# A four-layer hybrid encoder trunk: an attention order in which two steps share one PSUM tile, a last projection over the stored tokens alone, and four state buffers in the gated recurrence

## The reference, cut to what matters

```python
for i in range(DEPTH):                       # DEPTH = 4
    a = rms_norm(h, norm_mix_g[i])
    y = [mla_mixer, hgrn2_mixer, s5_mixer, retention_mixer][i](a, ...)
    h = h + y
    f = conv_glu_ffn(rms_norm(h, norm_ffn_g[i]), ...)   # 1024 -> 2*2816 -> conv -> silu*gate -> 1024
    h = h + f
return h[:, N_META:]                         # N_META = 16

# layer 0, per head: q, k, v from low-rank latents, q and k normalised over 192 columns
s = einsum(q_block, k) * scale;  s = where(mask, s, NEG_INF);  o = softmax(s) @ v
# layer 1, per head, in chunks: gated linear recurrence
state = state * exp(g_last) + k_tail^T v;    o = q_dec @ state + masked(q_dec k_inv^T) v
o = rms_norm(o, g_o) * silu(g)
```

## Time and profile before

| | us |
|---|---|
| median of three runs | 3178.77 |
| the profiled execution | 3176.39 |
| its span | 3174.6 |
| PE busy | 2892.7 (91%) |
| DVE busy | 2079.7 (66%) |
| POOL busy | 1319.7 (42%) |
| ACT busy | 977.1 (31%) |

### The profile page before, as it was taken

One profiled execution on the slowest core, in us unless ns is written; L12 is line 12 of the kernel. 1 busy time (PEld: TensorE's weight loads), 2 busy tenths in 40 slices (PEclk: granted clock), 3 DMA queues, 4 the chain that ended last, 5 costly groups with the idle time before them and its releaser, 6 DMA issues.

```text
span 3174.6 us, 59011 instructions
## 1 busy us (share of the span) xinstructions
PE 2892.7 (91%) x23040; PEld 2750.6 (87%) x23040; DVE 2079.7 (66%) x2743; ACT 977.1 (31%) x1403; POOL 1319.7 (42%) x603
## 2 busy tenths in 40 slices
PE   6778899999888879998965799999999999999999
PEld 6566799999888879998965799999999898899999
DVE  5676478861576757888969568884235435688840
ACT  3222233332334323332235333333212122222221
POOL 4111245564222224554453245555434243255553
PEclk8789899999999989999977899999999999999999
DMA  3100122233211112222310122223332222122232
GB/s 127 34 27 26 47 74 90 85 102 99 75 49 50 53 47 74 87 84 87 94 62 1 34 81 86 84 88 107 118 93 68 75 93 72 49 74 85 86 107 79
DMA packets 66412, 234.51 MB, mean 74 GB/s; under 512 B 8145, under 2 KB 8913, under 8 KB 65777
## 3 DMA queue, kind: packets, MB, share of 16 engines
q1 hardware_dynamic: 63648, 225.70, 23.3%
q10 hardware_dynamic: 2640, 7.02, 0.7%
HBM read 230.60 MB, written 2.10 MB: 73 GB/s over the span
## 4 chain that ended last, share of the span: by engine, by line
PE 50%; DVE 31%; issue 13%; ACT 2%; DVEq 2%; POOL 2%; DMA 0%; SPq 0%; ACTq 0%; POOLq 0%
PE ps L225 38%; DVE scr L445 7%; DVE scr L448 7%; DVE ub L439 4%; DVE scr L442 3%; PE ps L247 2%; PE ps L1893 1%; PE ps L1384 1%; ACT work L1688 1%; DVEq L442 1%; DVE work L1064 1%; DVE work L811 1%; PE ps L1009 1%; PE ps L238 1%; PE ps L1369 1%
## 5 line engine op out<-in xcount | busy, mean ns | idle before, releaser
L225 PE MATMUL ps<-xs,wr 128*128 128x264 f32 x13056 | 1646.5, 287 | 53.9 <-POOL wr L213 34.9
L213 POOL TENSOR_TENSOR wr<-raw,wr 128x1024 fp32r<-128x1024 f32 x422 | 1087.7, 2581 | 1441.5 <-ACT wr L205 1440.9
L225 PEld LDWEIGHTS ps<-xs,wr 128*128 128x128 f32 x13056 | 1612.7, 191 | 83.2 <-issue 51.6
L225 PE MATMUL ps<-hid,wr 128*128 128x264 f32 x6528 | 803.7, 286 | 25.4 <-POOL wr L213 17.6
L225 PEld LDWEIGHTS ps<-hid,wr 128*128 128x128 f32 x6528 | 798.8, 190 | 29.2 <-POOL wr L213 19.6
L205 ACT ACTIVATE wr<-raw 128x1024 fp32r<-128x1024 f32 x422 | 441.4, 1050 | 416.9 <-PE ps L225 413.1
L448 DVE SCALAR_TENSOR_TENSOR scr<-ub,convp,scr 128x528 f32<-128x528 f32 x176 | 448.1, 2546 | 24.0 <-DVE scr L445 0.6
L445 DVE SCALAR_TENSOR_TENSOR scr<-ub,convp,scr 128x528 f32<-128x528 f32 x176 | 228.9, 1301 | 26.6 <-DVE scr L442 17.5
L513 POOL TENSOR_TENSOR hid<-scr,hid 128x528 f32 x88 | 137.3, 1560 | 232.7 <-ACT hid L485 232.7
L464 DVE TENSOR_TENSOR h<-ps,h 128x528 f32<-128x528 f32 x32 | 22.6, 708 | 308.0 <-PE ps L225 307.8
L485 ACT ACTIVATE hid<-scr 128x528 f32 x88 | 56.8, 646 | 408.6 <-DVE scr L454 408.6
(11 more groups left out here) (249 smaller groups left out, 2263.3 us busy)
## 6 DMA issues: line engine op xcount, KB each, us to landing
raw<-in_stream SPq DMA_DIRECT2D x422, 512.0 KB, 3.6
work<-in_ret_tab ACTq DMA_DIRECT2D x4, 1056.0 KB, 5.3
h<-in_h SPq DMA_DIRECT2D x8, 264.0 KB, 6.0
out<-h SPq DMA_DIRECT2D x8, 256.0 KB, 4.5
work<-in_s_b ACTq DMA_DIRECT2D x1, 512.0 KB, 3.5
work<-in_s_c ACTq DMA_DIRECT2D x1, 512.0 KB, 4.6
convp<-in_convp ACTq DMA_DIRECT2D x4, 88.0 KB, 2.2
work<-in_mla_tab ACTq DMA_DIRECT2D x1, 264.0 KB, 2.5
```

The lines of the kernel that those rows point to most:

```text
L213: pool.tensor_tensor(wr[:, s, 1].rearrange("p a b -> p (a b)"), raw[:, s, :], wr[:, s, 0].rearrange("p a b -> p (a b)").bitcast(F32), ALU. ...
L225: mm = pe.matmul(out[:, q], wr[:, slot, w, b0 + k], x[k][v][:, q * HALF:(q + 1) * HALF], start=start and k == 0 and p == 0, stop=stop and ...
```

## The change: what it does, and the diff

- **Attention.** The value transposes leave `sum` and become a step `vt` of their own with a tile of their own, behind `spreadk`. `sum` moves from behind `O1` to right behind `("S", 4)`, and it writes into the tile of `("S", 4)`, whose scores lie in the first 16 columns (`tile_of`). `vv` moves behind `O1`. The loop keeps 22 tiles.
- **Recurrence.** Four state buffers in place of one. The update is a DVE operation that reads the new part straight from PSUM in `("S", b)`; the copy to `us` and the update in `("O", b)` go. The order is new: `OM` and the elementwise steps `e1'`, `e2'` come earlier, `q'` later, `e3'` ahead of `i'`, and `e4'` ahead of `Q`. The square on ACT is a step `sq`. PE sums the squares within `g'`, after 18 of its 48 matmuls (`SPLIT = 3`).
- **Last MLP.** Its down projection computes columns 16 to 527 alone, with one matmul of 512 columns where there were two of 264 (`project_real`).

```diff
+        def project_real(pe, out, slot, x, start, stop, inc, before):
+            for k in range(len(x)):
+                if k in before:
+                    pe.wait_ge(*before[k])
+                for p, (w, v) in enumerate(((0, 0), (0, 1), (1, 0))):
+                    mm = pe.matmul(out[:, 0:SEQ], wr[:, slot, w, k], x[k][v][:, META:T],
+                                   start=start and k == 0 and p == 0, stop=stop and k == len(x) - 1 and p == 2)
+            mm.then_inc(inc, 1)
...
+                        if last:
+                            project_real(pe, flat(gg + m), u % RING, x, j == 0, j == 2, unit_done, before)
...
-            P_SEQ = ["qn", "qr", "kn", "vv", "sum", "spreadq", "spreadk"]
+            P_SEQ = ["qn", "qr", "kn", "sum", "vv", "spreadq", "spreadk", "vt"]
...
-            X_SEQ = [("S", 0), ("S", 1), "qn", ("T", 0), ("S", 2), "qr", ("O", 0), "kn", ("T", 1), ("S", 3),
-                     "vv", ("T", 2), ("S", 4), ("O", 1), "sum", ("T", 3), ("O", 2), ("T", 4), "spreadq",
-                     "spreadk", ("O", 3), ("O", 4)]
+            X_SEQ = [("S", 0), ("S", 1), "qn", ("T", 0), ("S", 2), "qr", ("O", 0), "kn", ("T", 1), ("S", 3), ("T", 2),
+                     ("S", 4), "sum", ("O", 1), "vv", ("T", 3), ("O", 2), ("T", 4), "spreadq", "spreadk", "vt",
+                     ("O", 3), ("O", 4)]
+            def tile_of(seq, k):
+                return k - (seq is X_SEQ and k >= seq.index("sum"))
...
-                    pe.wait_ge(tile_free, g - 3 + i * W2)
+                    if s != "sum" or g < gX:
+                        pe.wait_ge(tile_free, g - 3 + i * W2)
...
+                    elif s == "vt":
+                        dve.wait_ge(p_pe.sem, p_pe.done("vt", h0) + i * 2 * len(p_pe.names))
+                        dve.tensor_copy(vt[j][:, 0:512], flat(g)[:, 0:512]).then_inc(p_dve.sem, p_dve.one("vt"))
+                        dve.tensor_copy(vt[j][0:META, 512:512 + P], flat(g)[0:META, 512:512 + P]).then_inc(tile_free, 1)
...
-            state = misc[:, 128:256]
-            us = [ub[:, 1, 130:258], ub[:, 1, 258:386]]
+            state = [misc[:, 128:256]] + [b_["ms"][:, QUARTER + k * P:QUARTER + (k + 1) * P] for k in range(QB - 1)]
...
-            P_SEQ = ["f", "q", "e1", "e2", "i", "e3", "e4", "g", "e5"]
-            X_SEQ = ["VK", "M", "f'", ("S", 0), "q'", "OM", "e1'", ("S", 1), ("O", 0), ("S", 2), "e2'",
-                     ("O", 1), ("S", 3), "i'", ("O", 2), "e3'", ("O", 3), "Q", "e4'", "g'", "N", "F", "e5'"]
+            P_SEQ = ["f", "e1", "e2", "q", "e3", "i", "e4", "g", "e5"]
+            X_SEQ = ["VK", "M", "f'", "OM", ("S", 0), "e1'", "e2'", "q'", ("S", 1), ("O", 0), ("S", 2), ("O", 1), ("S", 3),
+                     "e3'", "i'", ("O", 2), ("O", 3), "sq", "e4'", "Q", "g'", "N", "F", "e5'"]
...
+                    if r and s == "g":
+                        project(pe, tile(g), slot, 0, x[:SPLIT], True, False)
+                        squares(i, g)
+                        project(pe, tile(g), slot, SPLIT, x[SPLIT:], False, True, unit_done)
...
-                        dve.wait_ge(p_act.sem, p_act.done("Et", R))
+                        dve.wait_ge(p_act.sem, p_act.done("sigq", R))
...
                         if b < QB - 1:
                             masked.then_inc(a_dve.sem, a_dve.one(("mk", b)))
+                            dve.wait_ge(tile_free, g_of(("S", b - 1) if b else "OM", g) + 1 + i * PER)
+                            dve.scalar_tensor_tensor(state[b + 1], state[b], d128[:, b:b + 1], f[:, 512:640], ALU.mult, ALU.add)\
+                               .then_inc(tile_free, 1)
                             dve.wait_ge(a_dve.sem, a_dve.done(("mk", b), R))
-                            dve.tensor_copy(us[b % 2], f[:, 512:640]).then_inc(tile_free, 1)
...
-                        if b < QB - 1:
-                            dve.scalar_tensor_tensor(state, state, d128[:, b:b + 1], us[b % 2], ALU.mult, ALU.add)\
-                               .then_inc(a_dve.sem, a_dve.one(("st", b)))
```

More of the change, by code:

```diff
@@ L392, in setup_of, with ffn_pe @@
             return mixer[n].get("setup") if n in mixer else None
-        def ffn_pe(pe, n, layer, u0, g0):
+        def ffn_pe(pe, n, layer, u0, g0, last):
             x = split_tiles(xs, range(DT))
@@ L422, in ffn_pe @@
                         pe.wait_ge(lo_ready, u + 1 + i * 12)
-                        project(pe, tile(gg + m), u % RING, 0, split_tiles(hid, range(k0, k0 + nb)),
-                                j == 0, j == 2, unit_done, {k - k0: w for k, w in late.items()})
+                        x, before = split_tiles(hid, range(k0, k0 + nb)), {k - k0: w for k, w in late.items()}
+                        if last:
+                            project_real(pe, flat(gg + m), u % RING, x, j == 0, j == 2, unit_done, before)
+                        else:
+                            project(pe, tile(gg + m), u % RING, 0, x, j == 0, j == 2, unit_done, before)
                         k0 += nb
```

106 lines of the change are left out of this document (62 added, 44 removed).

## The result

| kernel | median, us (lowest to highest, runs) | profiled execution, us | its span, us | mean granted clock |
|---|---|---|---|---|
| before | 3178.68 (3175.6 to 3180.93, 4) | 3176.39 | 3174.6 | 0.951 |
| after | 3128.12 (3123.69 to 3135.3, 4) | 3125.63 | 3123.5 | 0.954 |

The ratio after to before is 0.9846, 95% interval 0.9827 to 0.9865: 50.6 us less in the medians (43 to 55 by the interval), where 35.5 were forecast. The time of 3128 lies inside the range of 3110 to 3160, but outside the forecast's own 3134 to 3150, on the side of more gain.

The account below looks back on a forecast made before the run. Attention and recurrence were taken as chains of waits between PE and DVE, the last down projection as PE alone. Gains of 9.1, 18.8 and 7.6 us made 35.5 off 3176.39: 3140.9, median 3143; own range 3134 to 3150, whole 3110 to 3160.

Parts of the forecast that it names:

- rival 2: Recurrence: the split stops the roots but the clock holds, 1.9 us per head more gain, 3130 us; chance 0.12.
- constant extra per matmul: Last down projection: 10.6 ns per matmul whatever its width, so 223.9 ns for 512 columns and 9.1 us less.
- upper bound: Last down projection: the extra grows with the columns, 233.9 ns per 512-column matmul and 3.8 us less.
- Rival 4: Last down projection: the 512-wide matmul doesn't stream, 0.85 ns per column, slower than before at 3254 us; chance 0.04.
- The roots' start: Attention loop: roots start 1.38 us behind block 3's probabilities, 2.85 us earlier in the mean.
- the tile wait: Attention loop: `spreadq` waits for the tile of `vv`, freed about 0.9 us later than before.
- `vt` cost: Attention loop: the two `vt` copies between `spreadk` and the next `S0` cost 0.4 us per head.
- half of the heads makes 0.5: Attention loop: half of the heads have their spreads at full clock, worth 0.5 us per head.
- Rival 5: Attention: the new order fails through the `vv` tile wait or `O1`, 0 to 0.5 us per head, 3153 us; chance 0.06.
- my walk: Recurrence loop: step-by-step timing of one head, 35.0 us before the split's hold on the roots is charged.
- Rival 1: Recurrence: the split doesn't stop the roots, heads of 35.0 us, gain 38.4 us, 3112 us; chance 0.13.
- Rival 3: Recurrence gains nothing: a second split or longer low clock, 7.6 to 12 us less gain, 3151 to 3155; chance 0.10.

Follow-up runs that it names:

- e9: Late round's kernel with `vv` again ahead of block 2's transposes in the attention loop; 3103.95 us.
- e4: Changed kernel with ACT rounding the gate's weight unit only behind the gate's sigmoid in the recurrence; 3113.53 us, ratio 0.9798 to the kernel before.
- e6: Changed kernel with 20 extra matmuls of 264 columns on PE ahead of its wait for the roots in the recurrence loop; 3121.48 us, ratio 0.9838.
- the late round: Changed kernel with the recurrence's gate weight unit rounded on ACT behind the gate's sigmoid, not ahead; 3113.53 us, and 3113.13 us when run again.

## Why the forecast was right in sign and place, and too small

The number alone would mislead: 3128 lies beside rival 2's 3130, and its distance to the forecast is made of errors of both signs.

1. **The last projection: the term was mis-sized.** I took a constant extra per matmul (223.9 ns, 9.1 us). The extra grows with the columns: 231.1 ns, 5.0 us measured, near my upper bound of 233.9 ns and 3.8 us. The choice of a constant was made without a row of another width in a stream of this type; the proportional bound was the nearer one. Rival 4 (0.85 ns per column) didn't happen: 0.45.
2. **Attention, the loop: 2.0 us per head forecast, 2.4 in the mean of six: 3.2 in a head of 31.0 us and 1.5 in one of 32.7.** The roots' start was right (1.28 us behind the copy against 1.38), the tile wait too (0.90 against 0.9). `vt` cost 0.05 instead of 0.4. The other step that was too small is "half of the heads makes 0.5": the spreads are at full clock in six of seven, in none without the cover of `vv`. By e9 that cover is worth 1.5 us against a head of 31.0, and 0.7 in the mean of six heads. The three heads of 32.5 to 32.9 us have the low level at other places (one of them at its spreads, which take 3.88 us); that wasn't in the sum. Rival 5 had nothing to it.
3. **Attention, the ends.** The first head gained 5.9 us (4.8 forecast). Up to its spreads it is 4.9 us, as forecast (they start 15.3 us behind the start of `turn` before and 10.4 after). The other 1.0 us lies behind them, where the low level lasts until 108.6 before and until 101.1 after; that this is the cause was not tried. From the last loop head to the output projection it was 6.1 where one head's 2.0 was forecast: in the trace before the last score blocks ran at the low level, in the one after at the full one. I didn't price that stretch at all.
4. **The recurrence loop: right by the mechanism, too small by 4.5 us.** Heads of 39.4 us in the mean of the first four intervals (forecast 39.4), a root operation held to the end of the split, a pause of 3.10 us (3.5). e4 and e6 take the two terms away one by one: 2.2 us for the split, 1.7 to 2.2 for the clock (2.3 and 1.9 forecast), and what is left is the 35.0 us of my walk. Rival 1 was worth what I had for it and didn't occur. Rival 2 occurred at one pause of seven, and with it the last two intervals are 37.9 and 38.1 us; without them the stage would have gained 8 us. The first head of the loop gained 2.4 us from its `VK` to its `N`. That makes 14.3 us for the loop against the 9.8 forecast. Rival 3 fell.
5. **The recurrence outside the loop: right for the first head, wrong by 1.2 us for the last.** The first head's projection lost 2.25 us (2.2 forecast): its `VK` starts 35.35 us behind the end of the down projection before (839.18 and 803.83) and 37.60 after (813.70 and 776.10). The last head lost 1.2 (0 forecast).
6. **Not in the sum:** the 4.1 us of the last up projections, and the 3.0 and 1.3 us of the other unchanged stretches. I took unchanged code for unchanged time. Two times 1.3 us of it are the clock that the changed mixers hand on; for the 4.1 us the cause is open, so that this part of the gain is luck.

Of the 15 us between 35.5 and 50.6, attention is 7.6, the recurrence 3.3 and the unchanged stretches 8.4, and the last projection takes 4.1 back.

Both kernels are beaten by the late round (3113.5 and 3113.1 us on two chips). The two versions built on it, with `vv` first and with extra matmuls in attention, have medians of 3104.0 and 3103.3 us (2.2% below the kernel before) and the smallest spreads of this family, 4 and 8 us.

## What to carry to other kernels

Taking away a stop pays only if what PE reaches next is ready as well: the state buffers alone gained nothing in the recurrence, since the square was not ready sooner. When an order is rewritten, look at what POOL does beside the chain that now sets the end: one split of 2.4 us, moved by one line on ACT, cost 3.9 us in the mean of six heads, about half of it as a held DVE operation and half as a lower clock behind PE's pause. Independent PE work beside the longest DVE chain can be worth a small tile wait (31.0 us against 32.5 per attention head at best), but look at several runs: here the order with the longer heads had no longer median. Code behind a changed stage can gain too, when the stage ends at a higher granted clock.

## What was not expected of the hardware

- The granted clock isn't a cost in itself: attention heads at 0.89 took 31.0 us, heads at 1.00 took 30.95, since the low level fell on matmuls that nobody waited for. Mean clock over a stage says little; which instructions run at the low level says it.
- Useless matmuls in a pause can pay: 1.7 us per head in the recurrence, nothing in the old attention order; in the new one the medians differ by 10 us, not clear of the spread.
- The same 3.10 us pause of PE was followed by the low level six times and once by full clock.
- 512 columns cost 231.1 ns, 17.8 above 512/2.4, and 264 columns 10.6 above 264/2.4.
- Code that isn't changed can take 4 us less or more; here it goes with how POOL's and DVE's rounds fall against each other.
